# Reordering the last block's chains, gates and table loads in a three-layer fp32 kernel

## What is computed

```python
h = rms_norm(x, g_pre) * (1 + scale) + shift            # scale, shift, gate from silu(c) @ w_ada
qkv_dn, z_dn, beta_logit, a_logit, qkv_mb, z_mb, merge_logit = split(h @ w_in)
qkv_dn = silu(causal_depthwise_conv(qkv_dn, conv_w))     # 4 taps
beta = sigmoid(beta_logit);  g = -exp(a_log) * softplus(a_logit + dt_bias)
a = strict(k_beta @ k.T * decay);  t_inv = inv(eye + a)           # gated delta rule, 4 heads of 128
u = t_inv @ v_beta;  w = t_inv @ (k_beta * exp(g));  qk = causal(q @ k.T * decay)
v_new = u - w @ state;  o = (q * exp(g)) @ state + qk @ v_new
y_dn = (rms_norm(o) * silu(z_dn)) @ w_proj_dn
o_mb = softmax(causal(q_mb @ k_mb.T / 8)) @ v_mb         # 8 heads of 64, one block of 256
y_mb = (o_mb * silu(z_mb)) @ w_proj_mb
x + gate * rms_norm((sigmoid(m_dn) * y_dn + sigmoid(m_mb) * y_mb) @ w_out, g_post)
```

## Time and profile before

| | before |
|---|---|
| median of the timed runs (3) | 931.89 us (931.8 to 932.09) |
| the profiled execution | 932.61 us |
| its span, first to last instruction | 930.8 us |
| PE busy | 897.8 us, 96% |
| DVE busy | 627.8 us, 67% |
| ACT busy | 482.8 us, 52% |
| POOL busy | 32.6 us, 4% |
| weights and constants read | 163.49 MB, 177 GB/s |

### The profile page before, as it was taken

How to read it: one execution, slowest core, us unless ns; L and a number is a source line. 1 busy time by engine, 2 the same in 40 slices (tenths; PEclk the granted TensorE clock), 3 DMA queues, 4 the chain that set the end, 5 groups by cost and what they waited for, 6 DMA issues and landing times.

```text
span 930.8 us, 14526 instructions
## 1 busy us (share of the span) xinstructions
PE 897.8 (96%) x6258; PEld 798.3 (86%) x6258; DVE 627.8 (67%) x758; ACT 482.8 (52%) x630; POOL 32.6 (4%) x25
## 2 busy tenths in 40 slices
PE   5999999999999999999999999999999999989997
PEld 4989888799999998988789999999889888877785
DVE  4798746578676666697567767677658594546555
ACT  7765456474333344755657333344656873337423
POOL 0000000000000000000000000000000244000000
PEclk9999999999999999999999999999998999999999
DMA  9554543366666664554345666665553343324331
GB/s 373 188 176 143 173 145 135 136 242 221 229 237 227 226 226 143 198 181 141 132 156 189 242 226 242 244 241 202 181 185 111 95 137 131 137 80 160 106 132 45
DMA packets 24016, 165.47 MB, mean 178 GB/s; under 512 B 2673, under 2 KB 2929, under 8 KB 4625
## 3 DMA queue, kind: packets, MB, share of 16 engines
q1 hardware_dynamic: 22320, 159.13, 48.6%
q0 software_dynamic: 1056, 4.34, 1.2%
q10 hardware_dynamic: 576, 1.08, 0.3%
HBM read 163.49 MB, written 1.05 MB: 177 GB/s over the span
## 4 chain that ended last, share of the span: by engine, by line
PE 83%; DVE 7%; ACT 7%; issue 1%; DMA 1%; DVEq 0%; SPq 0%; ACTq 0%
PE lin L517 15%; PE lin L519 14%; PE lin L518 14%; PE acc L517 10%; PE acc L518 10%; PE acc L519 10%; DVE w_lo L1725 3%; ACT w_hi L1271 3%; PE acc L747 1%; DMA raw<-in_weights 1%; PE acc L811 1%; PE lin L604 1%; PE lin L634 1%; ACT arena L1670 1%; ACT arena L1621 1%
## 5 line engine op out<-in xcount | busy, mean ns | idle before, releaser
L1725 DVE TENSOR_TENSOR w_lo<-raw,w_hi 128x2048 fp32r<-128x2048 f32 x138 | 319.7, 2326 | 156.7 <-ACT w_hi L1271 155.8
L1271 ACT CAST w_hi<-raw 128x2048 fp32r<-128x2048 f32 x138 | 262.2, 1905 | 170.1 <-DMA raw<-in_weights 107.7
L517 PE MATMUL lin<-h_hi,w_hi 128*128 128x256 f32 x736 | 211.3, 287 | 7.0 <-DVE h_lo L1771 2.7
L518 PE MATMUL lin<-h_lo,w_hi 128*128 128x256 f32 x736 | 209.1, 284 | 0.0
L519 PE MATMUL lin<-h_hi,w_lo 128*128 128x256 f32 x736 | 209.1, 284 | 0.0
L517 PEld LDWEIGHTS lin<-h_hi,w_hi 128*128 128x128 f32 x736 | 142.1, 193 | 8.7 <-DVE h_lo L1771 2.9
L518 PEld LDWEIGHTS lin<-h_lo,w_hi 128*128 128x128 f32 x736 | 142.1, 193 | 0.3
L519 PEld LDWEIGHTS lin<-h_hi,w_lo 128*128 128x128 f32 x736 | 142.0, 193 | 0.0
L517 PE MATMUL acc<-w_hi,f_hi 128*128 128x512 f32 x288 | 112.7, 391 | 0.0
L518 PE MATMUL acc<-w_lo,f_hi 128*128 128x512 f32 x288 | 112.2, 390 | 0.0
L519 PE MATMUL acc<-w_hi,f_lo 128*128 128x512 f32 x288 | 112.1, 389 | 0.0
(11 more groups left out here) (331 smaller groups left out, 1056.3 us busy)
## 6 DMA issues: line engine op xcount, KB each, us to landing
raw<-in_weights SPq DMA_DIRECT2D x150, 1024.0 KB, 4.9
rowbuf<-in_rows POOLq DMA_DIRECT2D x6, 512.0 KB, 4.5
x<-in_x_in SPq DMA_DIRECT2D x2, 512.0 KB, 4.6
arena<-in_const_even POOLq DMA_DIRECT2D x1, 1024.0 KB, 10.0
out<-x SPq DMA_DIRECT2D x3, 256.0 KB, 2.1
cst<-in_const ACTq DMA_DIRECT2D x1, 576.0 KB, 9.2
out<-x ACTq DMA_DIRECT2D x1, 256.0 KB, 2.1
colbuf<-in_cols ACTq DMA_DIRECT2D x1, 159.0 KB, 5.7
```

The lines of the kernel that those rows point to most:

```text
L517: pe.matmul(dst, st_hi, mv_hi, start=first, stop=False)
L518: pe.matmul(dst, st_hi, mv_lo, start=False, stop=False)
L1271: act.copy(w_hi[:, o % SPLIT, :], raw[:, j % RAW, :]).then_inc(hi_done, 1)
L1725: dve.tensor_tensor(w_lo[:, j % RAW, :], r, hi.bitcast(F32), ALU.subtract).then_inc(tile_split, 1)
```

## The change

The order of work and the place of some results change; what is computed does not.

- `last_lead`: the four quarters of dz go through `project_low_last`: of the 12 matmuls of a quarter the 8 with `w_hi` come first (they wait for `hi_done` alone), the 4 with `w_lo` last. `gates` becomes `gates(t)`, one token tile each: t = 0 ahead of dz's last quarter, t = 1 behind it. In the odd mixer likewise, around the last part of the lead product.
- ACT gets `load_root` and `load_exp`, one-element activations that bring the table in: ahead of the squares of each boundary, of the heads of the odd mixer and of the delta rule, and of the last residual; and ahead of dv's copy for the exponential of the decay matrix.
- ACT's exponential of `D` and the copy of beta go ahead of the taps, and the w_hi casts of bq's second tile and of bk's go between them. bq is copied out ahead of v's SiLU, X ahead of vb. On DVE the decay matrix goes ahead of bq's second w_lo, and `qk`, `at` ahead of qg and of bk's w_lo.
- On PE, bk's first half goes ahead of v's transposes, and `bk` and `dvt` change places in the list of PSUM pairs.
- In the delta rule the sums into acc stay open: the part of each sum that needs no late input is issued earlier, one start flag and one stop flag for the four heads of a bank.
- In the attention, ACT copies the transposed probabilities ahead of two casts, DVE does the gated products ahead of two w_lo, and `by` moves from a PSUM pair to acc, behind `mix_ready`; gm0 and gm1 so get different pairs.

The diff, cut to its core (semaphore declarations and passing `between` through `lead` are left out):

```diff
@@ -140,8 +140,8 @@
...
     g += ["n2a0", "n2a1", "dz", "*dk", "dq", "dv", "*drow", "*dbeta", "*dkt", "bq",
-          "*dvt", "bk", "bv", "bz", "gd0", "*gate", "gd1", "*dyt", "*bt0", "*bt1", "*bt2",
-          "gm0", "*by", "gm1", "*byt", "*y2a", "*y2b"]
+          "bk", "*dvt", "bv", "bz", "gd0", "*gate", "gd1", "*dyt", "*bt0", "*bt1", "*bt2",
+          "gm0", "gm1", "*byt", "*y2a", "*y2b"]
@@ -513,6 +515,10 @@
...
                 return w_hi[:, ORDINAL[n] % SPLIT, :], w_lo[:, n % RAW, :]
+            def high_tile(n):
+                pe.wait_ge(hi_done, ORDINAL[n] + 1)
+                return w_hi[:, ORDINAL[n] % SPLIT, :]
@@ -547,6 +553,24 @@
...
                         mm.then_inc(tile_used, 1)
+            def project_low_last(name, i, t):
+                if i == 0 and t == 0:
+                    open_pair(name)
+                n = FIRST[name] + i
+                hi = high_tile(n)
+                o = pair(name)[:, t * 512:(t + 1) * 512]
+                for k in range(4):
+                    for j, part in enumerate(chunk(4 * i + k)):
+                        pe.matmul(o, part[:, t * P:(t + 1) * P], hi[:, k * 512:(k + 1) * 512], start=i == 0 and k == 0 and j == 0,
+                                  stop=False)
+                lo = split_tile(n)[1]
+                for k in range(4):
+                    mm = pe.matmul(o, chunk(4 * i + k)[0][:, t * P:(t + 1) * P], lo[:, k * 512:(k + 1) * 512], start=False,
+                                   stop=i == 1 and k == 3)
+                if t == 1:
+                    mm.then_inc(tile_used, 1)
@@ -634,6 +658,16 @@
...
                 mm.then_inc(xt_done, 1)
+            def gates(t):
+                at = GATE_ACC["z"] + 16 * t
+                for k in range(DC):
+                    hi, lo = (part[:, k, t * P:(t + 1) * P] for part in (h_hi, h_lo))
+                    pe.matmul(acc[:, at:at + 16], hi, wg[:, k, :, :], start=k == 0, stop=False)
+                    mm = pe.matmul(acc[:, at:at + 8], lo, wg_hi[:, k, :], start=False, stop=k == DC - 1)
+                if t == TT - 1:
+                    mm.then_inc(gates_done, 1)
@@ -700,15 +736,18 @@
...
                 products(1, 0).then_inc(lead_done, 1)
-                project_token_major("dz", (0,), (0,))
+                project_low_last("dz", 0, 0)
...
-                project_token_major("dz", (1,), (0,))
+                project_low_last("dz", 1, 0)
...
-                project_token_major("dz", (0,), (1,))
+                project_low_last("dz", 0, 1)
...
-                project_token_major("dz", (1,), (1,))
+                after(wg_ready)
+                gates(0)
+                project_low_last("dz", 1, 1)
+                gates(1)
@@ -878,17 +917,6 @@
...
             mlp(0, first_turned(("n1a0", "n1a1"), 1))
-            def gates():
-                after(wg_ready)
...
-                mm.then_inc(gates_done, 1)
@@ -926,8 +954,11 @@
...
                 mm.then_inc(lin_special, 1)
-            lead("mq", ("n1a0", "n1a1"), 1)
-            gates()
+            def first_gates():
+                after(wg_ready)
+                gates(0)
+            lead("mq", ("n1a0", "n1a1"), 1, first_gates)
+            gates(1)
@@ -1061,12 +1091,12 @@
...
             fill("bq", 1)
+            fillers = [(n, i) for n in ("bk", "bv", "bz", "gd0") for i in range(2)]
+            fill(*fillers[0])
...
-            fillers = [(n, i) for n in ("bk", "bv", "bz", "gd0") for i in range(2)]
-            fill(*fillers[0])
@@ -1126,23 +1156,27 @@
...
             mm.then_inc(u_done, 1)
+            for h in range(H):
+                pe.matmul(acc[:, 1536 + h * P:1536 + (h + 1) * P], at("Y", P, h * T + P), at("vb", P, (H + h) * P),
+                          start=h == 0, stop=False)
...
+            for h in range(H):
+                pe.matmul(acc[:, h * P:(h + 1) * P], at("qk", P, h * T), at("v0", P, h * P), start=True, stop=True)
...
-                o = acc[:, 1536 + h * P:1536 + (h + 1) * P]
-                pe.matmul(o, at("Y", P, h * T + P), at("vb", P, (H + h) * P), start=True, stop=False)
-                mm = pe.matmul(o, at("wt", P, h * P), at("S", P, h * P), start=False, stop=True)
+                mm = pe.matmul(acc[:, 1536 + h * P:1536 + (h + 1) * P], at("wt", P, h * P), at("S", P, h * P),
+                               start=False, stop=h == H - 1)
...
+            for h in range(H):
+                pe.matmul(acc[:, 512 + h * P:512 + (h + 1) * P], at("qg", P, h * P), at("S", P, h * P), start=h == 0, stop=False)
...
-                pe.matmul(acc[:, h * P:(h + 1) * P], at("qk", P, h * T), at("v0", P, h * P), start=True, stop=True)
-                o = acc[:, 512 + h * P:512 + (h + 1) * P]
-                pe.matmul(o, at("qg", P, h * P), at("S", P, h * P), start=True, stop=False)
-                mm = pe.matmul(o, at("qk", P, h * T + P), at("v1", P, h * P), start=False, stop=True)
+                mm = pe.matmul(acc[:, 512 + h * P:512 + (h + 1) * P], at("qk", P, h * T + P), at("v1", P, h * P),
+                               start=False, stop=h == H - 1)
@@ -1173,7 +1207,7 @@
...
             fill("gm0", 0)
-            open_pair("by")
+            after(mix_ready, 2)
@@ -1181,17 +1215,17 @@
...
                         for b in range(2):
-                            o = pair("by")[64 * b:64 * b + 64, t * 512 + h * 64:t * 512 + (h + 1) * 64]
+                            o = acc[64 * b:64 * b + 64, t * 512 + h * 64:t * 512 + (h + 1) * 64]
...
-            mm.then_inc(lin_special, 1)
+            mm.then_inc(by_done, 1)
...
-            after(mix_ready, 2)
+            after(by_read)
@@ -1281,6 +1315,12 @@
...
                 act.activation(stat[:, 32:32 + s], stat[:, 16:16 + s], ACT.Sqrt).then_inc(sd_ready, 1)
+            def load_root():
+                act.activation(stat[:, 159:160], ident[:, 0:1], ACT.Sqrt)
+            def load_exp():
+                act.activation(stat[:, 159:160], ident[:, 0:1], ACT.Exp)
@@ -1327,6 +1367,7 @@
...
                 split_until(past(name, 2) if bias is None else LAST[name])
+                load_root()
@@ -1611,6 +1653,7 @@
...
             root_lengths()
+            load_exp()
@@ -1620,28 +1663,29 @@
...
                 ins.then_inc(taps_ready, 1)
-            taps(0)
-            taps(1)
+            after(w_diff_ready)
+            act.activation(at("D"), at("D"), ACT.Exp).then_inc(w_exp_ready, 1)
...
+            taps(0)
+            split_until(LAST["dv"] + 2)
+            taps(1)
...
+            split_until(LAST["dv"] + 3)
...
-            split_until(LAST["dv"] + 2)
-            after(w_diff_ready)
-            act.activation(at("D"), at("D"), ACT.Exp).then_inc(w_exp_ready, 1)
...
+            copy_out("bq", at("bq"), splits=False)
...
-            copy_out("bq", at("bq"))
+            split_until(LAST["bq"] + 3)
+            after(p_done)
+            for b in range(2):
+                ins = act.copy(low("X", b).rearrange("p (n t) -> p n t", n=8), own_blocks(acc[:, 0:1024], b))
+            ins.then_inc(X_ready, 1)
...
-            split_until(LAST["bq"] + 4)
-            after(p_done)
-            for b in range(2):
-                ins = act.copy(low("X", b).rearrange("p (n t) -> p n t", n=8), own_blocks(acc[:, 0:1024], b))
-            ins.then_inc(X_ready, 1)
@@ -1669,10 +1714,10 @@
...
             ins.then_inc(be_ready, 1)
-            ahead("dn_out")
...
+            ahead("dn_out")
@@ -2319,27 +2365,26 @@
...
             dve.engine_nop().then_inc(kbg_ready, 1)
+            after(w_exp_ready)
+            d8 = at("D").rearrange("p (n t) -> p n t", n=8)
+            link(dve.tensor_tensor(d8, d8, over_blocks(const_of("causal")[:, 0:P]), ALU.mult))
+            read_out(dve, "dbeta")
+            link(dve.tensor_tensor(at("at"), at("D"), at("beta"), ALU.mult))
...
+            after(sc_done)
+            dve.tensor_tensor(at("qk"), at("D"), acc[:, 1024:2048], ALU.mult)
+            dve.tensor_tensor(at("at"), at("at"), acc[:, 0:1024], ALU.mult).then_inc(at_ready, 1)
...
-            after(w_exp_ready)
-            d8 = at("D").rearrange("p (n t) -> p n t", n=8)
-            link(dve.tensor_tensor(d8, d8, over_blocks(const_of("causal")[:, 0:P]), ALU.mult))
-            read_out(dve, "dbeta")
-            link(dve.tensor_tensor(at("at"), at("D"), at("beta"), ALU.mult))
...
-            after(sc_done)
-            dve.tensor_tensor(at("qk"), at("D"), acc[:, 1024:2048], ALU.mult)
-            dve.tensor_tensor(at("at"), at("at"), acc[:, 0:1024], ALU.mult).then_inc(at_ready, 1)
...
-            ahead("bq")
-            split_until(LAST["bq"] + 4)
+            split_until(LAST["bq"] + 3)
@@ -2389,17 +2434,16 @@
...
                     dve.tensor_tensor(mix, mix, sig, ALU.add).then_inc(mix_ready, 1)
-            ahead("dn_out")
...
-            filled(dve, "by")
+            after(by_done)
...
-            dve.tensor_tensor(y16, pair("by")[:, :].rearrange("p (n d) -> p n d", d=64), inv, ALU.mult).then_inc(freed("by"), 1)
```

(18 more changed lines are left out.)

## The result

| | before | after |
|---|---|---|
| median of the timed runs | 931.99 us (931.8 to 933.13, 4 runs) | 922.38 us (920.74 to 923.17, 4 runs) |
| ratio, 95% interval | | 0.9892 (0.9875 to 0.9909) |
| the profiled execution | 932.61 us | 923.17 us |
| its span | 930.8 us | 921.4 us |

What follows compares the result with a forecast made beforehand. PE's stream was taken to set the time, busy 897.8 of 930.8 us. Waits removed and a clock fall avoided, less one new wait, summed to 15.0 us: 916.9 us forecast, range 914.2 to 921.8.

Steps and rivals of the forecast that it cites:

- part 1: Square-root tables loaded early: PE waits shrink at two boundaries (1.6 us), odd mixer's heads (0.5), behind the delta rule (0.9).
- part 7: Attention: bt0's wait of 1.74 us shrinks to about 0.35 (gain 1.55), the wait for gm0's sigmoid goes (1.3).
- Part 2: dz's two tiles: low parts last remove PE's waits of 1.18 and 0.51 us for w_lo; gain 1.7 us.
- part 3: Gates by token tile: low clock at the last block's gates and the half projection behind goes; gain 3.0 us.
- Part 5: New PE wait at bv's first half, for ACT's copy of bk out of a shared PSUM buffer; cost 1.7 us.
- Part 6: Open sums of the delta rule: fillers remove waits of 0.78, 0.68 and 0.87 us; gain 2.8 us.
- overlap of 0.16 us per wait: Matmuls overlap by 0.16 us in a running stretch, so each wait that goes was taken to gain 0.16 us more.
- part 4: bq, dvt, bk: PE's waits of 0.35, 1.96 and 1.50 us go; new lateness 0.3 and 0.45; net 3.3 us.
- rival (b): DVE's run beside GpSimd is later than thought, by 2 to 5 us: 918.9 to 921.9 us; chance 0.15.
- Rival (a): Clock still falls once, at gates(0) behind transposes or at the new wait for bk's copy; 3 us, 919.9; chance 0.15.

Runs made afterwards that it cites:

- r2_after_again: The changed kernel as it is, timed again in five executions: 922.32 us, ratio 0.9871 to the kernel before.
- g1: The kernel before with the early square-root table loads alone: 930.67 us, ratio 0.9962 to the kernel before.
- g2: The kernel before with the open sums of the delta rule alone: 930.27 us, ratio 0.997 to the kernel before.
- e4: Changed kernel with bk copied out ahead of Pm, and parts of bq's second and bk's first tile ahead of taps and decay matrix: 920.59 us.
- f4: Changed kernel with bk copied out ahead of Pm, w_lo products of bq and bk behind those with w_hi, qg behind Y: 917.09 us.

## Why the prediction was wrong

The stretches between equal products of PE, before against r2_after_again (which had the fall at 421 alone), put a number on each part. Starts of the products are taken from the two timelines.

| up to | before | after | gain | forecast |
|---|---|---|---|---|
| first product behind the odd mixer's gates | 408.00 | 407.20 | 0.80 | 0.79 (part 1) |
| odd mixer's heads | 454.06 | 454.26 | -1.00 | 0.5 (part 1) |
| beta turned (L714, L753 after) | 731.47 | 726.49 | 5.18 | 5.49 (parts 1 to 3) |
| bt0 (L1173, L1207 after) | 860.95 | 852.16 | 3.81 | 6.85 (parts 1, 4 to 7) |
| last w_lo wait | 915.21 | 905.02 | 1.40 | 1.3 (part 7) |

**Right.** Part 1: the waits went at each boundary, 0.6 us of the heads' and the 0.77 us behind the delta rule. In time each boundary gave 0.65 us and not 0.79: of the first row's 0.80 us 0.15 are there at 22 us already, ahead of any edit (the same product starts at 22.74 and at 22.59 us); at the second, PE needs 27.14 us from the heads to the transposes of x before (454.06 to 481.20) and 26.48 us after (454.26 to 480.74). Part 2 and part 3 in this pair of executions: 4.5 of 4.7 us. Part 5: 1.65 us of wait for 1.7. Part 6 alone: 2.7 for 2.8. Part 7: bt0's wait 0.23 us for a forecast 0.35, gm1's gone. The overlap of 0.16 us per wait is borne out nowhere: the boundaries gave what their waits lasted, and g1's 2.65 us of waits brought 2.1 to 2.3 us.

**Wrong, 3.0 us: the lateness in part 4.** The three old waits went as said (3.8 us), but I put the new lateness of bq's and bk's w_lo at 0.3 and 0.45 us; it was 2.01 and 1.72. The price that I used for a w_lo beside GpSimd's adds, 2.93 us, came from one that overlapped the adds by its first 0.8 us only (742.35 against an end at 743.13). In the changed order DVE's run and the three adds start together, and a w_lo costs 4.54 us, 2.25 more than alone; qg costs 1.6 more and the second w_lo 0.95 more. Parts 4 and 5 together were to gain 1.6 us. By the table the fourth row lacks 3.04 us of its forecast; with the other parts of that row confirmed, they cost 1.4. The rival (b) was this mechanism, at 2 to 5 us; I gave it a chance of 0.15 only because I priced DVE's run from the one meeting that was short. "SBUF — State Buffer" of the Trainium skill, section "SBUF: two separate sides", calls the shared port pair an exclusive lock and not a split of bandwidth, and names among DVE's instructions those with two SBUF inputs. Here the trace agrees as to which instructions suffer (those that read SBUF alone; 1.21 us as ever for the two that read PSUM as well), and the extra 2.25 us is near one whole add (2.03 us, half of the earlier trace rows's first). A w_lo that starts together with an add so costs itself and about one add, which is the price that I should have taken.

**Wrong, 2.3 us between the profiled executions: part 3's 3.0 us were booked as if the clock stayed up everywhere else.** Part 3 is right where it looks: 691 to 705 us at 1.00 in every profile with split gates. But I summed against one execution, as if its falls were the kernel's. In the kernels with whole gates there are two places where the clock may fall behind them, 388 and 698 us; the execution on the page had the second, g1 and g2 both. Kernels with the early root tables may fall at 16 and fell in every profile at 421 us; the three kernels without them fell at neither. (g2 and e4 fell once more, at 746 and 755 us, each behind a wait of PE of 2 us.) The change takes the chance of the first two away. The changed kernel's profiled execution had the other two. The fall at 16 us costs 0.75 us; that at 421 costs 1.6, the 1.00 us of the table's second row and the 0.6 us of wait that went there. Sum: 15.0 - 3.0 - 2.3 = 9.7 us forecast in hindsight, 9.4 measured between the profiled executions. What the change is worth without any fall of the clock can be read too: 929.8 us (two runs at 0.999) against 921.1 (0.999 and 1.0), 8.7 us; the sum without part 3 and with the true lateness gives 15.0 - 3.0 - 3.0 = 9.0. The 0.3 us left over are of the size by which the overlap was taken too large. Rival (a), a fall that stays, had about the right size and the wrong place.

The transposes beside gates(0) did not make a fall: 691 to 698 stays at 1.00. "TensorE: Matmul & The Clock Gate" of the Trainium skill, Part 4, says that transposes do not count as a busy PE; the prediction took from it that the clock might fall here, and in none of the seven profiles with split gates did it. That does not refute the sentence of the page: the whole gates of the odd mixer, 3.49 us of narrow products, are a longer stretch than these 2.7 us, and they too ran at 1.00.

**Open.** Why the clock falls at 388 us in one execution and at 698 in another is not settled; each place was only seen to fall or not. Open too is whether the early root tables bring the fall at 421 us; no profile of a kernel with them is without it. If they do, 1.6 of the 2.3 us are a cost of part 1 and not chance. It is also open which of the two smaller edits of f4 beside the low parts, qg behind Y or bk's early copy, its last microsecond needs. Moving the adds to another engine wasn't tried.

## What to carry to other kernels

Before moving DVE work next to a GpSimd instruction, price every SBUF-only instruction of the run as if each first met a whole one of GpSimd's, and not by an average row; where such a run can't be shortened, let PE do first what doesn't need its result (f4's 4 us of high parts hid 3.7 us of waits at no cost). When a kernel's clock falls in a few places by chance, collect the clocks of all timed runs first, and forecast an edit that removes such a fall at its chance times its price: the one execution gave 3.0 us, the medians 1.9.

## What the runs showed of the hardware

- A w_lo of 128 x 2048 on DVE took 2.29 us alone, 3.2 beside the masks and 4.54 beside the tap adds of GpSimd; a 128 x 512 product 0.68 and 2.29 us. GpSimd's adds suffer too: three took 8.48 us, 2.83 each, where two had taken 4.06.
- The same program has a mean clock of 0.988 to 0.999 from one execution to the next, and 929.8 to 936.3 us with it. The mean is not enough to sort executions: at 0.990 the kernel before took 933.77 and 936.13 us. It also counts what costs nothing: in r2_after_again the clock stood at 0.50 from 918 to 920 us, behind PE's last product.
- A one-element activation ahead of the squares brings the root's table in and it stays: no load came between it and the root, and the 0.63 us waits went (g1).
